# Modulation and normalised input of a decoder layer: one stage instead of two

## The reference

```
mod = (silu(c) @ w_ada + b_ada)            # c: 9 rows (1 prompt, 8 sequences)
sh1, sc1, ga1, sh2, sc2, ga2 = split(mod, 6)
h = rmsnorm(x, g_pre1) * (1 + sc1) + sh1   # x: 512 + 64 rows of 1024
parts = h @ w_in                           # the projections
```

## Time and profile before

| | us |
|---|---|
| median of three runs | 2636.57 |
| lowest, highest | 2635.83, 2647.21 |
| the profiled execution's own time | 2642.91 |
| its span | 2641.1 |

### The profile page before, as it was taken

How to read it: one execution, slowest core, us unless ns; L and a number is a source line. 1 busy time by engine, 2 the same in 40 slices (tenths; PEclk the granted TensorE clock), 3 DMA queues, 4 the chain that set the end, 5 groups by cost and what they waited for, 6 DMA issues and landing times.

```text
span 2641.1 us, 24928 instructions
## 1 busy us (share of the span) xinstructions
PE 2226.0 (84%) x8970; PEld 1258.3 (48%) x8970; DVE 1233.0 (47%) x3186; ACT 698.1 (26%) x2115; POOL 730.0 (28%) x694
## 2 busy tenths in 40 slices
PE   6999989997787999878888887979788777787786
PEld 2777447865575776344443443434344333333221
DVE  1000001225232011457767667676776776767764
ACT  2000012332120001223333333333333443333322
POOL 0000001110101000034444443535444444454441
PEclk8999989997676999989999998989899898898899
DMA  7566648978672125079999999999999999999997
GB/s 279 228 252 253 249 142 303 318 307 333 222 270 104 60 72 179 4 281 420 416 418 417 413 419 409 420 406 420 410 418 412 415 421 404 420 415 414 418 418 301
DMA packets 134914, 850.41 MB, mean 322 GB/s; under 512 B 15121, under 2 KB 32817, under 8 KB 52989
## 3 DMA queue, kind: packets, MB, share of 16 engines
q0 software_dynamic: 85760, 691.32, 64.5%
q1 hardware_dynamic: 47740, 154.95, 15.9%
q10 hardware_dynamic: 1290, 2.55, 0.3%
HBM read 836.43 MB, written 99.37 MB: 354 GB/s over the span
## 4 chain that ended last, share of the span: by engine, by line
DMA 18%; PE 18%; DVE 17%; issue 2%; ACT 2%; POOL 1%; ACTq 0%; POOLq 0%
DMA pr_ring<-in_uv,pr_idx 18%; PE ps L1718 17%; DVE pr_ring L1859 4%; POOL pr_ring L1670 1%; DVE pr_hot L1843 1%; DVE pr_hot L1839 1%; DVE pr_ind L1820 1%; DVE pr_ind L1817 1%; DVE pr_pick L1846 1%; PE ps L1684 1%; ACT pr_coef L1777 1%; DVE pr_val L1819 1%; DVE pr_rest L1818 1%; DVE pr_val L1816 1%; DVE pr_pos L1820 1%
## 5 line engine op out<-in xcount | busy, mean ns | idle before, releaser
L1718 PE MATMUL ps<-pr_ring,pr_diag 128*128 128x512 f32 (+1 forms) x2304 | 1084.4, 626 | 288.9 <-ACT pr_diag L1781 288.5
L1670 POOL DMA_INDIRECT pr_ring<-in_uv,pr_idx x576 | 658.3, 1143 | 1129.1 <-PE ps L1718 761.4
L1859 DVE CUSTOM_DVE_ANT_0 pr_ring<-pr_ring,h 128x1024 f32<-128x1024 f32 x576 | 691.5, 1225 | 435.3 <-DMA pr_ring<-in_uv,pr_idx 428.4
L1718 PEld LDWEIGHTS ps<-pr_ring,pr_diag 128*128 128x128 f32 (+1 forms) x2304 | 438.4, 195 | 896.0 <-issue 510.2
L1772 ACT ACTIVATE pr_gel<-pr_dots 128x2 f32<-128x2 f32 x288 | 58.3, 202 | 637.5 <-DVE pr_dots L1859 637.3
L1781 ACT ACTIVATE pr_diag<-ident,pr_coef 128x128 f32<-128x128 f32 x512 | 173.5, 386 | 0.0
L1777 ACT ACTIVATE pr_coef<-pr_gel,pr_wgt 128x1 f32<-128x1 f32 x576 | 138.6, 287 | 27.6 <-ACT pr_gel L1772 1.1
L1415 PE MATMUL ps<-trunk,mg_ring 128*128 128x288 f32 x512 | 129.2, 412 | 12.6 <-DMA mg_ring<-in_w_merge 12.6
L1684 PE MATMUL ps<-trunk,pr_wq 128*128 128x192 f32 (+1 forms) x512 | 132.1, 412 | 2.3 <-PEq L1480 1.3
L430 PE MATMUL ps<-trunk,ap_ring 128*128 128x288 f32 x384 | 126.3, 411 | 2.9 <-PEq L323 2.9
L431 PE MATMUL ps<-trunk,ap_ring 128*128 128x288 f32 x384 | 125.2, 408 | 0.0
(11 more groups left out here) (289 smaller groups left out, 2036.4 us busy)
## 6 DMA issues: line engine op xcount, KB each, us to landing
out_win_s<-in_cache POOLq DMA_DIRECT2D x64, 1020.0 KB, 7.9
sa_ring<-in_cache SPq DMA_DIRECT2D x24, 1024.0 KB, 7.7
late_ring<-in_w_ada SPq DMA_DIRECT2D x8, 2048.0 KB, 17.6
sa_ring<-in_kcacheB SPq DMA_DIRECT2D x16, 1024.0 KB, 7.6
out_win_s<-in_cache POOLq DMA_DIRECT2D x16, 1008.0 KB, 10.7
ap_ring<-in_w_attn_qk SPq DMA_DIRECT2D x6, 2048.0 KB, 11.4
mg_ring<-in_w_merge SPq DMA_DIRECT2D x16, 768.0 KB, 4.2
sa_ring<-in_kcacheA SPq DMA_DIRECT2D x8, 1280.0 KB, 5.9
```

What stands on the lines that cost most here:

```text
L1670: pool.indirect_dma_start(ring[:, n % RING, :], None, d["uv"], bass.IndirectOffsetOnAxis(ap=idx[:, b % 4, j:j + 1], axis=0)).then_inc(arri ...
L1718: mm = pe.matmul(ps[0:r, bank + half, :], diag[:, n % RING, 0:r], ring[:, n % RING, o:o + CHUNK], start=h == 0 and j == 0, stop=b == FINAL ...
L1859: ins = dve.tensor_tensor_reduce(u, u, e.h2[:, BLOCKS[b][0], :], 1.0, 0.0, ALU.mult, ALU.add, dots[:, n % RING:n % RING + 1])
```

## The change

The two functions become one, `modulated_input`, one block. 

- SP issues everything with no wait: cT, x, the sample's x, the four chunks in the order 0, 2, 1, 3 (shift and scale of the first 512 channels, then of the last 512) into four slots, then the three projection weights. ScalarE's queue has only constants.
- A chunk's eight products go to four column groups (two slices of 128 rows added up in each), with weights of 32 columns, so that PSUM holds four partial sums on 128 partitions. VectorE copies them as they are (`take`). `fold` multiplies each 128-column piece of that copy by `fold9`, a 128x9 matrix of zeros and ones; that adds up the four partial sums and turns the result in one product.
- TensorE's order is: chunk 0, chunk 1, turning x, fold 0 and 1, chunk 2, chunk 3, fold 2 and 3. The turning no longer needs the factors: ScalarE copies the turned slices plain (8 copies), and the factors are applied in place afterwards, for each half of the channels two slices by ScalarE and two by VectorE.
- VectorE's order is: copy of chunk 0, 1/rms, scaling x, copy of chunk 1, factors of the first half (3 operations), first half of prompt and sample, copies of chunks 2 and 3, and the second half. The sample's part takes two operations of 256 columns for each half.

```diff
--- before.py
+++ after.py
@@ -110,6 +110,7 @@
         "c_restart": f(np.tile(restart, (H, 1))), "c_sel": f(sel.reshape(H, H * P)),
         "c_block": f((seq[:, None] == np.arange(NS)[None, :])),
         "c_fold": f(np.tile(np.eye(TS), (P // TS, 1))),
+        "c_fold9": f(np.tile(np.eye(32)[:, :NC], (4, 1))),
         "c_iota": f(np.tile(np.arange(TOPK), (P, 1))),
     }
@@ -153,41 +154,48 @@
-def modulation(nc, k, d, n):
-    NCK = 2 * D // CHUNK
+def modulated_input(nc, k, d, n, held):
+    ORDER = (0, 2, 1, 3)
+    HALF = KD // 2
+    x = n.x
     with ExitStack() as ctx:
         sb = lambda n, s, dt=F32: ctx.enter_context(nc.sbuf_tensor(n, s, dt))
-        wring = sb("ada_ring", [P, NR, KD, CHUNK])
+        w = sb("ada_w", [P, len(ORDER), KD, CHUNK])
         cT = sb("ada_cT", [P, KD, NC])
-        mod = sb("ada_mod", [NC, 2, D])
-        bias = sb("ada_bias", [NC, 2, D])
+        part = sb("ada_part", [P, len(ORDER), CHUNK])
+        fold9 = sb("ada_fold9", [P, NC])
+        bcol = sb("ada_bcol", [P, 2, KD])
         gcol = sb("ada_gcol", [P, KD])
         junk = sb("ada_junk", [P, D])
         ms = sb("ada_ms", [P, NCH])
         rt = sb("ada_rt", [P, NCH])
-        ready = [k.sem(f"ada_w_ready{r}") for r in range(NR)]
-        s_c, s_b, s_pad, s_silu, s_mm, s_add, s_tr, s_chain, s_const, s_x, s_sq, s_ms, s_rt = (
-            k.sem("ada_" + name) for name in ("c", "bias", "pad", "silu", "mm", "add", "tr", "chain", "const",
-                                              "x", "sq", "ms", "rt"))
+        ready = [k.sem(f"ada_w_ready{r}") for r in range(len(ORDER))]
+        s_c, s_pad, s_silu, s_mm, s_part, s_fold, s_mod, s_chain, s_ident, s_const, s_x, s_sq, s_ms, s_rt, s_xn, s_tr, s_ev, s_in, s_shift = (
+            k.sem("ada_" + name) for name in ("c", "pad", "silu", "mm", "part", "fold", "mod", "chain", "ident", "const", "x",
+                                              "sq", "ms", "rt", "xn", "turned", "taken", "input", "shift"))
         ps = k.ps
+        SAMPLE, FOLD, TURN = 2, 3, 4
         with nc.Block() as block:
             @block.sync
             def _(sp):
                 sp.dma_start(cT[:], d["cT"]).then_inc(s_c, 16)
-                for w in range(NCK):
-                    if w >= NR:
-                        sp.wait_ge(s_mm, w - NR + 1)
-                    sp.dma_start(wring[:, w % NR], d["w_ada"][w]).then_inc(ready[w % NR], 16)
+                sp.dma_start(x[:, 0:PT, :], d["x_prompt"].rearrange("(t p) n -> p t n", p=P)).then_inc(s_x, 16)
+                sp.dma_start(x[0:TS, PT, :], d["x_sample"]).then_inc(s_x, 16)
+                for at, chunk in enumerate(ORDER):
+                    sp.dma_start(w[:, at], d["w_ada"][chunk]).then_inc(ready[at], 16)
+                for r in range(held.slots):
+                    sp.dma_start(held.w[:, r], d["w_attn_qk"][r]).then_inc(held.ready[r], 16)
+                held.loaded = held.slots
             @block.scalar
             def _(act):
-                act.dma_start(bias[:].rearrange("p a n -> p (a n)"), d["b_ada"].partition_broadcast(NC)).then_inc(s_b, 16)
-                act.dma_start(n.x[:, 0:PT, :], d["x_prompt"].rearrange("(t p) n -> p t n", p=P)).then_inc(s_x, 16)
-                act.dma_start(n.x[0:TS, PT, :], d["x_sample"]).then_inc(s_x, 16)
-                for dst, src in ((k.ident, "c_ident"), (k.sel, "c_sel"), (k.block, "c_block"), (k.fold, "c_fold"),
-                                 (k.iota, "c_iota"), (gcol, "g_pre1")):
+                act.dma_start(k.ident[:], d["c_ident"]).then_inc(s_ident, 16)
+                for dst, src in ((fold9, "c_fold9"), (bcol, "b_ada"), (gcol, "g_pre1"), (k.sel, "c_sel"),
+                                 (k.block, "c_block"), (k.fold, "c_fold"), (k.iota, "c_iota")):
                     act.dma_start(dst[:], d[src]).then_inc(s_const, 16)
                 act.wait_ge(s_c, 16)
                 act.wait_ge(s_pad, 1)
@@ -195,59 +203,121 @@
                 act.wait_ge(s_x, 32)
                 for i in range(NCH):
                     r = tile_rows(i)
-                    act.activation(junk[0:r], n.x[0:r, i, :], ACT.Square, accum_out=n.ss[0:r, i:i + 1]).then_inc(s_sq, 1)
+                    act.activation(junk[0:r], x[0:r, i, :], ACT.Square, accum_out=n.ss[0:r, i:i + 1]).then_inc(s_sq, 1)
                     act.wait_ge(s_sq, i + 1)
                 act.wait_ge(s_ms, 2)
                 act.activation(rt[:, 0:PT], ms[:, 0:PT], ACT.Sqrt)
                 act.activation(rt[0:TS, PT:NCH], ms[0:TS, PT:NCH], ACT.Sqrt).then_inc(s_rt, 1)
+                for c in range(KD):
+                    act.wait_ge(s_tr, c + 1)
+                    act.activation(k.hT[:, c, 0:SEQ], ps[:, TURN + c % 4, :], ACT.Copy).then_inc(s_ev, 1)
+                act.wait_ge(s_ev, KD)
+                for half in range(2):
+                    act.wait_ge(s_mod, half + 1)
+                    for c in (half * HALF, half * HALF + 1):
+                        ins = act.activation(k.hT[:, c, 0:SEQ], k.hT[:, c, 0:SEQ], ACT.Identity, scale=k.scale1[:, c, 0:1],
+                                             bias=k.shift1[:, c, 0:1])
+                ins.then_inc(s_in, 1)
+                act.wait_ge(s_in, 1)
             @block.tensor
             def _(pe):
+                def chunk(at):
+                    pe.wait_ge(ready[at], 16)
+                    if at >= 2:
+                        pe.wait_ge(s_part, at - 1)
+                    for step in range(2):
+                        for j in range(4):
+                            c = 2 * j + step
+                            mm = pe.matmul(ps[32 * j:32 * j + 32, at % 2, :], k.cs[:, c, :], w[:, at, c, :],
+                                           start=step == 0, stop=step == 1)
+                    mm.then_inc(s_mm, 1)
+                def fold(at):
+                    pe.wait_ge(s_part, at + 1)
+                    for b in range(HALF):
+                        o = (at * HALF + b) * NC
+                        mm = pe.matmul(ps[:, FOLD, o:o + NC], part[:, at, b * P:(b + 1) * P], fold9[:], start=True, stop=True)
+                    mm.then_inc(s_fold, 1)
                 pe.wait_ge(s_silu, 1)
-                for w in range(NCK):
-                    pe.wait_ge(ready[w % NR], 16 * (w // NR + 1))
-                    if w >= 2:
-                        pe.wait_ge(s_add, w - 1)
-                    for c in range(KD):
-                        mm = pe.matmul(ps[0:NC, w % 2, :], k.cs[:, c, 0:NC], wring[:, w % NR, c, :],
-                                       start=c == 0, stop=c == KD - 1)
-                    mm.then_inc(s_mm, 1)
-                pe.wait_ge(s_add, NCK)
-                pe.wait_ge(s_const, 96)
-                for a in range(2):
-                    for c in range(KD):
-                        mm = pe.transpose(ps[:, 2 + a, c * NC:(c + 1) * NC], mod[:, a, c * P:(c + 1) * P],
-                                          k.ident[0:NC, 0:NC])
-                mm.then_inc(s_tr, 1)
+                chunk(0)
+                chunk(1)
+                pe.wait_ge(s_ident, 16)
+                pe.wait_ge(s_xn, 1)
+                for c in range(KD):
+                    if c >= 4:
+                        pe.wait_ge(s_ev, c - 3)
+                    for i in range(PT):
+                        pe.transpose(ps[:, TURN + c % 4, i * P:(i + 1) * P], x[:, i, c * P:(c + 1) * P], k.ident[:])
+                    pe.transpose(ps[:, SAMPLE, c * TS:(c + 1) * TS], x[0:TS, PT, c * P:(c + 1) * P],
+                                 k.ident[0:TS, 0:TS]).then_inc(s_tr, 1)
+                pe.wait_ge(s_const, 112)
+                fold(0)
+                fold(1)
+                chunk(2)
+                chunk(3)
+                pe.wait_ge(s_mod, 1)
+                fold(2)
+                fold(3)
             @block.vector
             def _(dve):
                 chain = Chain(dve, s_chain)
+                def take(at):
+                    dve.wait_ge(s_mm, at + 1)
+                    dve.tensor_copy(part[:, at, :], ps[:, at % 2, :]).then_inc(s_part, 1)
+                def modulation(half):
+                    cs = slice(half * HALF, (half + 1) * HALF)
+                    dve.wait_ge(s_fold, 2 * half + 2)
+                    src = lambda a: ps[:, FOLD, (2 * half + a) * HALF * NC:(2 * half + a + 1) * HALF * NC].rearrange(
+                        "p (c n) -> p c n", n=NC)
+                    dve.tensor_tensor(k.shift1[:, cs, :], src(0), broadcast_mid(bcol[:, 0, cs], NC, 2), ALU.add)
+                    chain.step(dve.tensor_tensor(k.scale1[:, cs, :], src(1), broadcast_mid(bcol[:, 1, cs], NC, 2), ALU.add))
+                    dve.tensor_tensor(k.scale1[:, cs, :], k.scale1[:, cs, :], broadcast_mid(gcol[:, cs], NC, 2),
+                                      ALU.mult).then_inc(s_mod, 1)
+                    dve.wait_ge(s_mod, half + 1)
+                def prompt(half):
+                    for c in (half * HALF + 2, half * HALF + 3):
```

(45 more changed lines are left out.)

37 lines of the change are left out of this document (removed).

## The result

| | kernel before | changed kernel |
|---|---|---|
| median (20 runs each) | 2645.2 us | 2632.6 us |
| lowest, highest | 2629.5, 2655.1 | 2613.9, 2643.1 |
| ratio | | 0.9949, 95% interval 0.9928 to 0.9969 |

A forecast was written before the change was run, and what follows sets the result against it. The first projection product's start was taken to bound the kernel; loads, chunks, normalising, turning, folds and tail summed to 49.9 us instead of 60.7, a gain of 10.8, median 2625.8 us (0.41% less), range 2614 to 2634.

The forecast's parts named there:

- Start: Projections onward: TensorE runs without gaps, so whatever the first projection product (60.68 us before) gains, everything behind it gains.
- Loads: First loads on SP's queue: x second, landing near 9 us, chunk 0 at 14.0 us (bounds 13.0 and 16).
- Chunks: Chunk products: four column groups run side by side, chunk 0 taking 3.4 us at the low clock, ending at 17.4.
- Rival 2: Chunk products: column groups don't overlap at 512 columns; 3.8 us slower than before, 2640.4 us; chance 0.05.
- Normalising: VectorE between chunk 0 and turning: copy, means, root, reciprocals and scalings now on the path, from 17.4 to 24.0 us.
- Turning: 40 transposes of x at clock 0.50: 10.8 us, ending at 34.8; bounds 10.8 low, 6.2 high.
- Folds, chunks 2 and 3: TensorE after the turning: folds 0 and 1 3.8 us, chunk 2 3.4, chunk 3 2.2, ending at 44.2 us.
- Tail: From chunk 3's end to first projection product: copy, fold 3, small operations, scalings, sample operations; 5.7 us, ending at 49.9.
- Sum: Whole new stage: first projection product at 49.9 instead of 60.7 us, 10.8 us gained, median 2625.8 us, 0.41% less.
- Rival 1: New stage: clock high from the turning on, 10.8 us more gain, 2615.0 us; chance 0.13.
- Rival 3: New stage: data or small steps later, chunk 0 at 16 us; about 5 us less gain, 2630.5 us; chance 0.22.
- Rival 4: Behind the new stage: start earlier but a later stage waits anyway; gain 0 to 3 us, 2635 us; chance 0.05.

The follow-up runs named there:

- x_other_queue: Changed kernel with x back on ScalarE's queue, issued first there, constants behind it; ratio to the kernel before 1.0013, first projection product at 60.0 us.
- one_group: Changed kernel without column groups, a chunk's eight products all adding up in partitions 0 to 31; ratio to the kernel before 1.0012, first projection product at 60.7 us.
- norm_first: Changed kernel with VectorE's means, reciprocals and scalings ahead of the copy of chunk 0; ratio to the kernel before 0.9901, first projection product at 41.0 us.
- fill: Changed kernel with extra unused products in TensorE's idle time (26 before chunk 0, 5 after it, 5 after chunk 1); one execution, first projection product at 42.1 us.
- fill_norm_first: Changed kernel with extra products and normalising before chunk 0's copy, run twice; ratios to the kernel before 0.9914 and 0.9900, first projection product at 41.0 and 41.2 us.
- before_kept_warm: Kernel before with six extra unused 512-column products behind the 16 small transposes; one execution, turning 6.4 us, first projection product at 57.6 us.
- after_again: Changed kernel, unedited, profiled a second time; ratio to the kernel before 0.9942, first projection product at 49.9 us.
- chunk1_late: Changed kernel with chunk 1's products behind the turning of x in TensorE's order; ratio to the kernel before 0.9964, first projection product at 50.0 us.

## Why the prediction was right, and where it was not

- **Start.** Coverage of the stage behind: right. What the new stage gains arrives at the prompt attention (17.2 of 18.4; 1.2 are lost as the projections' own start was longer at the low clock) and passes the last stage untouched.
- **Loads.** Mechanism right (x first is needed: x_other_queue), size wrong: x by 1.7 to 2.6 us and chunk 0 by 1.6 to 2.4. I priced the constants' small packets at 1 us. In the first 10 us of the changed kernel ScalarE's queue passed 617 packets for 0.09 MB, where before it had 140, and the whole moved 277 GB/s, not the 312 of the earlier trace rows:

```profile
q1 hardware_dynamic: 769, 2.67, 80.9%
q10 hardware_dynamic: 617, 0.09, 5.9%
```

  With the constants behind x (x_other_queue) the first 10 us moved 309 GB/s, which speaks for the small packets as the cause. But the difference, 0.35 MB, is only about 0.8 us. The sum also had no time between a transfer's last packet and its use: in the first profile x's last packet ended at 9.7 us and the squares began at 10.7, chunk 0's last packet ended at 15.1 and its products began at 15.6.

- **Chunks.** 3.6 us at the low level, 1.9 at the high one: four groups overlap nearly fully at 512 columns too. At the high clock one_group's 32 records, 0.43 us apart, make 13.8 us against 3.6, 3.8 times (its 15.6 hold 3.4 us at the low clock). Rival 2 falls, and the 2.38 times that the Trainium skill ("TensorE: Matmul & The Clock Gate", Part 3) gives for three tiles is no guide to four: here it is 3.8 times. The 0.2 us that I read for two changes of tiling also holds the last product's own time; no run here prices such a change.
- **Normalising.** 6.4 us for 6.6. That chunk 0's copy stands in front was seen and counted; that it was worth removing was not said.
- **Turning.** The term that decides. "At most the first 2 us of the turning are fast; I take 10.8" came true in three of four profiles of the changed kernel (10.4, 9.6 and 9.6 us; a part of the first slice fast in one, two slices in two) and failed in the one that was shown first (6.3 us). I read the earlier trace rows as a property of transposes. It is one of what ran before: low they stay low, high they stay high if products run up to them (norm_first, fill, both fill_norm_first and one_group with no gap, before_kept_warm with 0.8 us: six of six high); with a gap of 1.5 to 1.7 us it stayed high once and fell in the third slice twice; with a gap of 3.2 us it fell in the first slice, and with 6 us or more it was low from the start. The Trainium skill ("TensorE: Matmul & The Clock Gate", Part 4) says that a transpose does not count as busy in the way a product does; that transposes don't raise the clock agrees, but a clock that stayed high for 6 to 8 us over nothing else is more than this says. one_group shows that even without a gap it does not always stay: it fell 9.4 us after chunk 1's last product, 1.2 us into chunk 2.
- **Folds, chunks 2 and 3.** 3.6 us at the low clock for 3.8 counted; chunks 5.3 to 6.3 for 5.6 where the turning was low.
- **Tail.** 4.9 us instead of 5.7: fold 3 ran at the high clock (0.12 a record), 1.0 us for 1.4; the rest is in the small steps.
- **Sum.** In the low case the errors cancel: in after_again the turning starts 1.9 us late, then the turning (0.4), the folds (0.3), chunks 2 and 3 (0.4) and the tail (0.8) each take less than counted. 49.9 to 50.7 against 49.9 is right in its mechanism, the low clock; the agreement to the tenth is luck. Against the kernel before's 60.7 and 62.1 that is about 11 us, and about 19 in the high case. Three of the one and one of the other would make 13 us, close to the ratio's 13.5; how often each comes in unprofiled runs was not measured, and the interval of 8 to 19 us can't tell.
- **Rival 1** came in one of four profiles, at 42.3 us where its own count gives 40.7, for the late start.
- **Rival 3** held for the data (late), not for the result. **Rival 4** falls.

What stays open: why a gap of 1.5 us once kept the clock and gaps of 1.6 us twice did not. One more thing differs between these profiles: where the clock stayed, all of chunk 1 had the low clock's spacing (3.64 us), so the high clock began only behind it; in the two others it began within chunk 1 (3.48 and 3.49 us). No run here was made to vary the gap, or the moment at which the clock rises, finely.

## What to carry to other kernels

Before a step is moved, ask what TensorE does right ahead of it in the new order: the same 40 transposes cost 6.3 or 9.6 to 10.4 us in the changed kernel. A gap of 1.5 to 3 us ahead of them, which VectorE's order of work had made, put the clock at risk, and closing it by that order did as much, by time, as adding products. Where single runs scatter by 1%, judge an edit of a stage by the start of the next stage in several profiles: the first pair showed 29 us, of which the edit had made 18, and in three further profiles the edit made about 11.

## What the runs showed of the hardware that was not expected

- Transposes do not raise a low clock (10.7 to 10.8 us at 0.50 in before, chunk1_late and x_other_queue), and 40 of them did not lose a high one when products ran up to them (6.3 to 6.4 us, six profiles of five kernels).
- 16 records with 128 columns of weights and 9 moving take 1.95 us at the high clock and 3.6 at the low one.
- Small constants on the second queue seem to slow large loads on the first: with 617 packets of 0.09 MB beside x the first 10 us moved 277 GB/s, with the constants behind x 309.
- The middle of this kernel (mLSTM) takes 153.8 to 175.4 us in the four profiles of the changed kernel, by its clock. That is 20 to 22 of the 28 to 30 us between the first profile's span and the other three.
